# Packing the small experts of a mixture-of-experts layer, and one unsplit fp32 weight piece in six

## The reference

```
logits = h @ w_router + b_router                  # (256, 8)
top_logit, top_idx = top_k(logits, 2);  top_w = softmax(top_logit)
# for each expert e, over the rows xb of the tokens that chose it:
y_e = (silu(xb @ w1[e]) * (xb @ w3[e])) @ w2[e]   # w1, w3: 1024 x 3584, w2: 3584 x 1024
y[token] += top_w * y_e
```

## Time and profile before

| what | value |
|---|---|
| median of three runs | 1914.64 us |
| span of the profiled execution | 1919.3 us (no other time was recorded for it) |
| mean granted TensorE clock, share of full speed | 0.953 |
| TensorE matmuls busy | 1731.4 us, 90% |
| VectorE busy | 1421.4 us, 74% |
| ScalarE busy | 1042.3 us, 54% |
| read from HBM | 500.50 MB, 261 GB/s over the span |
| the experts' part | from 725.81 us to about 1900 us of the span |

### The profile page before, as it was taken

One profiled execution on the slowest core, in us unless ns is written; L12 is line 12 of the kernel. 1 busy time (PEld: TensorE's weight loads), 2 busy tenths in 40 slices (PEclk: granted clock), 3 DMA queues, 4 the chain that ended last, 5 costly groups with the idle time before them and its releaser, 6 DMA issues.

```text
span 1919.3 us, 22270 instructions
## 1 busy us (share of the span) xinstructions
PE 1731.4 (90%) x7882; PEld 1390.2 (72%) x7883; DVE 1421.4 (74%) x1201; ACT 1042.3 (54%) x817; POOL 25.5 (1%) x31
## 2 busy tenths in 40 slices
PE   1899979996999949989979989999899899999995
PEld 0787758885877727868868868887687687787784
DVE  7776877757676776877868866656588688787787
ACT  1465434433555326757747745554577576675773
POOL 0100000000000000000000000000000000000000
PEclk9998989998999969999999999999999999999998
DMA  9874458754665436987978965666599699799892
GB/s 367 309 271 144 154 186 315 275 182 171 249 214 179 145 115 240 357 327 274 362 288 306 363 253 197 219 219 219 180 354 380 236 362 363 278 359 344 300 362 83
DMA packets 210686, 503.98 MB, mean 263 GB/s; under 512 B 9137, under 2 KB 13409, under 8 KB 210481
## 3 DMA queue, kind: packets, MB, share of 16 engines
q1 hardware_dynamic: 208770, 496.15, 72.3%
q0 software_dynamic: 1712, 5.43, 0.9%
HBM read 500.50 MB, written 1.05 MB: 261 GB/s over the span
## 4 chain that ended last, share of the span: by engine, by line
PE 79%; DVE 10%; issue 8%; ACT 2%; DMA 1%; DVEq 0%; ACTq 0%; SPq 0%
PE ps L1241 22%; PE ps L1243 22%; PE ps L1242 22%; DVE w_lo L772 2%; PE ps L1247 2%; PE ps L1248 2%; PE ps L1644 2%; PE ps L1530 2%; PE ps L1686 1%; DVE mod_acc L797 1%; ACT w_hi L457 1%; DVE stats L817 1%; PE ps L1365 1%; DVE gates L966 1%; PE ps L1366 1%
## 5 line engine op out<-in xcount | busy, mean ns | idle before, releaser
L772 DVE TENSOR_TENSOR w_lo<-w_raw,w_hi 128x2048 fp32r<-128x2048 f32 x423 | 966.4, 2291 | 381.7 <-ACT w_hi L457 381.1
L457 ACT CAST w_hi<-w_raw 128x2048 fp32r<-128x2048 f32 x423 | 806.5, 1910 | 352.0 <-PE ps L1243 282.7
L1241 PE MATMUL ps<-w_hi,actT_hi 128*128 128x512 f32 (+1 forms) x1536 | 613.8, 400 | 60.0 <-issue 40.2
L1243 PE MATMUL ps<-w_hi,actT_lo 128*128 128x512 f32 (+1 forms) x1536 | 600.0, 391 | 0.0
L1242 PE MATMUL ps<-w_lo,actT_hi 128*128 128x512 f32 (+1 forms) x1536 | 599.4, 390 | 0.0
L1241 PEld LDWEIGHTS ps<-w_hi,actT_hi 128*128 128x128 f32 x1536 | 294.3, 192 | 132.3 <-issue 60.9
L1243 PEld LDWEIGHTS ps<-w_hi,actT_lo 128*128 128x128 f32 x1536 | 293.3, 191 | 61.6
L1242 PEld LDWEIGHTS ps<-w_lo,actT_hi 128*128 128x128 f32 x1536 | 294.8, 192 | 57.5 <-issue 1.0
L1241 PE MATMUL ps<-w_hi,gT_hi 128*128 128x512 f32 x536 | 213.1, 398 | 16.3 <-DVE gT_lo L1058 14.1
L1243 PE MATMUL ps<-w_hi,gT_lo 128*128 128x512 f32 x536 | 213.6, 398 | 0.0
L1242 PE MATMUL ps<-w_lo,gT_hi 128*128 128x512 f32 x536 | 213.2, 398 | 0.0
(11 more groups left out here) (225 smaller groups left out, 1070.3 us busy)
## 6 DMA issues: line engine op xcount, KB each, us to landing
w_raw<-in_exp_w_dram SPq DMA_DIRECT2D x336, 1024.0 KB, 7.0
w_raw<-in_ffn_w_dram SPq DMA_DIRECT2D x33, 1024.0 KB, 5.2
w_raw<-in_w_mod_mix_dram SPq DMA_DIRECT2D x24, 1024.0 KB, 8.1
w_raw<-in_w_mod_ffn_dram SPq DMA_DIRECT2D x24, 1024.0 KB, 5.3
w_raw<-in_w_gate_dram SPq DMA_DIRECT2D x24, 1024.0 KB, 5.7
w_raw<-in_w_in_dram SPq DMA_DIRECT2D x14, 1024.0 KB, 7.3
w_raw<-in_w_out_dram SPq DMA_DIRECT2D x8, 1024.0 KB, 5.1
w_raw<-in_w_branch_c_dram SPq DMA_DIRECT2D x4, 1024.0 KB, 5.0
```

What stands on the lines that cost most here:

```text
L457: nc.scalar.copy(w_hi[:, j % SPLIT, :], w_raw[:, i % RING, :]).then_inc(split_hi, 1)
L772: TTn(w_lo[:, j % SPLIT, :], w_raw[:, i % RING, :], w_hi[:, j % SPLIT, :].bitcast(F32), ALU.subtract).then_inc(piece_used, 1)
L1241: MM(to, hi, w_h, start=first, stop=False)
L1243: return MM(to, lo, w_h, start=False, stop=last)
```

## The change

- An expert of at most 64 rows gets one packed block (`fb=0`): the code for the folded block, before only for the second of two blocks, takes the block's number `fb`.
- In such an expert the second B piece of each panel (`WHOLE`, pieces 3, 7, 13, 19, 25, 31 and 37) is not split: TensorE multiplies w_raw itself, as fp32, by x_whole = x_hi + x_lo (64 columns and 64 zeros), four matmuls (`up_whole`). x_whole lies in mod_acc, is made by VectorE at the expert's start, and stands ahead of `packed_ready`, for which TensorE waits.
- SyncE waits for `split_used`, raised by TensorE, ahead of each load that goes into the slot of a `WHOLE` piece, in every expert.
- The gather of a second block moves from the end of the expert before into the expert's own start, and its branch on the next count is gone. A branch on a count of at most 64 is added.

```diff
+WHOLE = {i for i, piece in enumerate(EXPERT.pieces) if piece[0] == "B" and piece[2] == 1}
...
+        x_whole = mod_acc[:, 0:KD * P].rearrange("p (k q) -> p k q", k=KD)
...
             def stream(stretch, base, layer, expert=None, mod_layer=None, gap=0):
...
+                    if stretch is EXPERT and (i - RING) % EXPERT.n in WHOLE:
+                        sp.wait_ge(split_used, expert * EXPERT.n_split + (moe_splits + i - RING + 1 + SPLIT))
+                        load(i % RING, piece, layer, expert)
+                        continue
...
# ScalarE (VectorE alike)
-                    def round_expert_piece(i, e):
-
+                    def round_expert_piece(i, e, whole=()):
+                        if i in whole:
+                            return
+                        count = 2 if i - 1 in whole else 1
...
-                    def second_block(e, n):
-                        with act.If(act.value_load(counts_i[0:1, bass.ds(e, 1)], min_val=0, max_val=SEQ) > P):
-                            gathered_rows(1, n)
-                        with act.Else():
-                            act.sem_inc(xg_hi_ready[1], 1)
...
+                            if blocks == 2:
+                                gathered_rows(1, e + 1)
+                            else:
+                                act.sem_inc(xg_hi_ready[1], 1)
...
# VectorE
+                    dve.wait_ge(gate1_ready, 4)
+                    nc.vector.memset(x_whole[:, :, HALF_P:P], 0.0)
...
-                                dve.wait_ge(xg_hi_ready[1], e + 1)
-                                dve.wait_ge(xg_lo_ready[1], e + 1)
-                                nc.vector.tensor_copy(actT_hi[:, :, P + HALF_P:2 * P], actT_lo[:, :, P:P + HALF_P].bitcast(F32)).then_inc(packed_ready, 1)
+                                dve.wait_ge(xg_hi_ready[fb], e + 1)
+                                dve.wait_ge(xg_lo_ready[fb], e + 1)
+                                at = fb * P
+                                ins = nc.vector.tensor_copy(actT_hi[:, :, at + HALF_P:at + P], actT_lo[:, :, at:at + HALF_P].bitcast(F32))
+                                if fb == 0:
+                                    ins = TTn(x_whole[:, :, 0:HALF_P], actT_hi[:, :, 0:HALF_P].bitcast(F32), actT_lo[:, :, 0:HALF_P].bitcast(F32), ALU.add)
+                                ins.then_inc(packed_ready, 1)
...
# TensorE
+                    def up_whole(i, h):
+                        for k in range(4 * h, 4 * h + 4):
+                            ins = MM(bank(HW3), x_whole[:, k, :], w_raw[:, i % RING, (k % 4) * BANK:(k % 4 + 1) * BANK], start=k == 0, stop=k == KD - 1)
+                        return ins
...
-                        pe.wait_ge(piece_used, piece_base + i + 1 + RING)
+                        whole = fb == 0 and i in WHOLE
+                        if whole:
+                            pe.wait_ge(raw_loaded[i % RING], e * EXPERT.landed[i % RING] + (moe_loads[i % RING] + stretch.loads[i]))
+                        else:
+                            pe.wait_ge(piece_used, piece_base + i + 1 + RING)
...
-                        def expert(blocks, packed=False):
-                            if packed:
+                        def expert(blocks, fb=None):
+                            pe.wait_ge(xg_hi_ready[0], e + 1)
+                            pe.wait_ge(xg_lo_ready[0], e + 1)
+                            if blocks == 2:
+                                gather(1, e + 1)
+                                pe.wait_ge(xg_hi_ready[1], e + 1)
+                                pe.wait_ge(xg_lo_ready[1], e + 1)
+                            else:
+                                pe.sem_inc(gathered_hi[1], 1)
+                                pe.sem_inc(gathered_lo[1], 1)
+                            if fb is not None:
                                 pe.wait_ge(packed_ready, e + 1)
...
-                            expert(1)
+                            with pe.If(count > HALF_P):
+                                expert(1)
+                            with pe.Else():
+                                expert(1, fb=0)
```

More of the change, by code:

```diff
@@ L173 @@
 FOLDS = 2 * len(EXPERT_PANELS)
+WHOLE = {i for i, piece in enumerate(EXPERT.pieces) if piece[0] == "B" and piece[2] == 1}
+assert EXPERT.n - 1 not in WHOLE and not WHOLE & set(range(SPLIT))
 LOGITS = 64
@@ L631, in _, with panel_events @@
                                             sbase + MIX.n_split))
-                def panel_events(stretch, panels, split_base, panel0, blocks, folds=None):
+                def panel_events(stretch, panels, split_base, panel0, blocks, folds=None, fb=None):
+                    whole = [b for b in range(blocks) if b != fb]
                     first_b = {stretch.split_no[i]: p[1] for i, p in enumerate(stretch.pieces) if p[0] == "B" and p[2] == 0}
@@ L643, in gT_part @@
                         for b in range(blocks):
-                            n = HALF_P if b and folds is not None else P
+                            n = HALF_P if b == fb else P
                             ins = A(gT_hi[:, b, 0:w // P, 0:n], ps[:, HW1 + 2 * b, 0:w].rearrange("p (c q) -> p c q", q=P)[:, :, 0:n], ACT.Copy)
@@ L655, in after @@
                             if folds is not None:
-                                A(fold[:, 0, 0:w], ps[HALF_P:P, HW1 + 2, 0:w], ACT.Copy).then_inc(fold_copied, 1)
-                            for b in range(1 if folds is not None else blocks):
+                                A(fold[:, 0, 0:w], ps[HALF_P:P, HW1 + 2 * fb, 0:w], ACT.Copy).then_inc(fold_copied, 1)
+                            for b in whole:
                                 ins = A(silu[:, b, 0:w], ps[:, HW1 + 2 * b, 0:w], ACT.Silu)
@@ L1082, in after @@
                                 dve.wait_ge(fold_added, folds + 2 * p + 2)
-                                ins = TTn(gated[0:HALF_P, 1, 0:w], silu[0:HALF_P, 1, 0:w], fold[:, 1, 0:w], ALU.mult)
+                                ins = TTn(gated[0:HALF_P, fb, 0:w], silu[0:HALF_P, fb, 0:w], fold[:, 1, 0:w], ALU.mult)
                             ins.then_inc(gated_ready, 1)
@@ L1219, in _ @@
                             with dve.Else():
-                                expert(2, packed=True)
+                                expert(2, fb=1)
                         with dve.Else():
-                            expert(1)
+                            with dve.If(count > HALF_P):
+                                expert(1)
+                            with dve.Else():
+                                expert(1, fb=0)
                     dve.wait_ge(added, 4 * EXPERTS + 4)
@@ L1520, in _, with swiglu @@
                 open_sublayer(layer * 2 + 1, 0, 4)
-                def swiglu(stretch, panels, piece_base, panel0, blocks, e=None, turn_places=None, packed=False):
+                def swiglu(stretch, panels, piece_base, panel0, blocks, e=None, turn_places=None, fb=None):
                     def turn(p):
@@ L1527, in turn @@
                         for b in range(blocks):
-                            n = HALF_P if b and packed else P
+                            n = HALF_P if b and b == fb else P
                             for c in range(panels[p] // P):
@@ L1546, in down @@
                             for n in range(2):
-                                ins = (packed_product if b and packed else product)(
+                                ins = (packed_product if b == fb else product)(
                                     bank(2 * b + n), gT_hi[:, b, k, :], gT_lo[:, b, k, :], *split_piece(j, c, n * BANK, D),
```

90 lines of the change are left out of this document (39 added, 51 removed).

## The result

The changed kernel takes 1965.38 us (median of four, 1961.73 to 1967.34) where the kernel before takes 1914.67 (1905.44 to 1916.42) on the same chip: a ratio of 1.0275, 95% interval 1.0246 to 1.0304. That is slower, and past the range of the prediction. The profiled spans are 1965.7 and 1919.3 us: 46.3 us to explain.

The account below looks back on a forecast made before the run. It took TensorE to set the pace, with VectorE's ring next in small experts. Terms -21 + 12 + 4 + 1 = -4 us took the profile from 1919.3 to 1915, or 1911 us from the median; range 1888 to 1939.

Parts of the forecast that it names:

- Added at the loop's turn: Start of each small expert: TensorE waits for VectorE's turn, copy and x_whole, some 7.4 us idle; +12 us in all.
- rival 2: Start of each small expert: VectorE comes round late, in 10.79 us instead of 4.89; +27, 1938 us; chance 0.14.
- The removed branch: Loop's turn: dropping the second block's branch saves between nothing and 5.9 us of ScalarE's turn; taken as nothing.
- Expert 3: Start of the two-block expert: second gather now stands behind TensorE's turn; +4 us, bounds +1 and +6.
- SyncE's wait: Loads into a whole piece's slot, every expert: SyncE waits for that piece's product, later loads behind it; +1 us.
- The ring: Panel of a small expert: ScalarE's handshake, VectorE and one TensorE piece set a 16.43 us period, gaining 0.56 a panel.
- Rivals 3 and 4: Small experts' panels: transfers hold them at 16.99 us, 1928, chance 0.13; or more overlap shortens them to 15.7, 1890, chance 0.15.
- The small expert: Each of five experts of at most 64 rows: 4.2 us saved, -21 us together.
- The start: Small expert, restart until the end of panel 1's second A piece: 16.4 us after that loss-laden beginning; gain 1.8.
- The panels: Small expert, five periods to panel 6: gain 2.8 us, less 1.2 for the token picks.
- The end: Small expert's last panel from the second A on: 20.1 us before, 20.2 after; gain taken as 0.8.
- rival 1: Small experts' panels: TensorE's gaps lower the granted clock once a panel; +39, 1950 us; chance 0.08.

Follow-up runs that it names:

- Run 2: The changed kernel with its test count > HALF_P made count > 0, so the third body stays in the code but is never taken: 1963.59 us, ratio 1.0242.
- run 5: The changed kernel without its third body, all experts of up to 128 rows using the ordinary one-block body; later second gather and SyncE's wait stay: 1937.35 us.
- run 12: The changed kernel with packing in the previous expert's tail, the loop's closing branch announced and the small body tested for first: 1895.84 us, ratio 0.9895.
- run 14: The kernel of run 12 with VectorE's picks of the next expert's tokens moved from the middle panel to the tail: 1886.92 us, ratio 0.984.

## Why the prediction was wrong

**The failed step is "Added at the loop's turn".** It gave the small experts +12 us (its five costs add up to 12.6); their idle times, 25.4 us before (2.56, 8.20, 4.86, 7.02 and 2.73), are 68.6 now, +43, of which 40 are loss (expert 0 starts only 3.4 us later, though its idle time grew by 6.7). Two prices were wrong in it.
- *VectorE's turn.* "VectorE took 4.89 us to come round to the same copy before expert 3". That row was not near enough: expert 3's body comes early in the code, and that turn had two far jumps, 2.75 and 1.97 us. The way to a small expert has three, the first of them longer; the same copy follows the last addition after 12.49 us. This is the mechanism of rival 2, which had the right place and, at 1938, a price 27 us too low. It took ScalarE's turn of 10.79 us as the worst case, and that was a turn of a kernel with one body fewer.
- *TensorE's own turn.* It had no term at all. I took its idle times as a property of the loop that the change leaves alone. Run 2 shows 12.5 us with nothing of the change in use but the third body. With early packing TensorE's own way is 9.4 to 13.2 us, so even a VectorE that came round in 4.89 us would not have saved the forecast.

The two far jumps of VectorE on its way into expert 3, from the chain of waits of the kernel before:

```profile
1139.07 2.75 issue
...
1142.71 1.97 issue
```

Of the 50 us between the forecast's -4 and the 46.3 of the trace, 28 are this step at the small experts, 16 the small experts themselves, 4 expert 3 and 2 experts 1 and 6.

The rows to price it were in the trace: ScalarE's 10.79 us and TensorE's 8.20 us "waiting for nothing that the profile shows" each stood behind taken branches, and the queues of instructions were on the page.

**The removed branch** of the second block was priced at nothing, since it was ScalarE's. In run 5, which lacks it, the short gaps are gone; that the one is the cause of the other is not shown. Why the kernel before has gaps of 2.7 and 2.9 us at some turns and 7 to 8 at others, with the same path through the code, isn't settled; the former need one block of code for TensorE and the latter three.

**Expert 3**: +4 forecast, 5.5 measured in the gap (10.2 to 15.7, the gather cold at 7.08 us, as its upper bound had it) and 2.8 in the expert itself. **SyncE's wait**: +1 forecast, about nothing measured.

**The ring** held as a mechanism. With 0 at 1045.24, the forecast put the silu at 1.55, the first split at 2.08, VectorE's at 4.02, gT at 6.23 and TensorE's first C at 6.78; the trace has 1.54, 2.08, 4.06, 6.27 and 6.83. The whole piece takes 3.60 us, where 3.65 was forecast. The period is 16.75 instead of 16.43 us: VectorE's multiplication waits 0.2 us for its own fold, and the eight matmuls of a piece take 0.1 us more behind a gap. So the gain is 0.24 us a period, not 0.56. Rivals 3 and 4 are out: the transfers run at 388 GB/s in such a panel, no engine waits there for a landing, and no panel was shorter than 16.7.

**The small expert**: -4.2 us each forecast, -1.0 measured. I cut the five where the prediction cut them, at the end of the second A piece of panel 1 and of panel 6.
- The start holds: -8.6 us, where -9 was forecast. It takes 16.5 to 17.6 us, and 15.0 where the turn is clean (run 12, experts 2, 5 and 7), against the 16.4 forecast.
- The panels are 3.2 us longer instead of 8 shorter. The period gives 0.24 us and not 0.56; the first one takes 17.3 us, since VectorE adds the fold of panel 1 only after other work (the silu is 2.1 us behind the end of the A piece there, not 1.54); and the picks cost 1.2 us in two experts and 2.4 in three, where 1.2 was forecast, the rest by the clock. Before, they were not hidden either: that panel took 17.7 us instead of 17.0.
- The end is 0.3 us longer instead of 4 shorter.

With the turn and the picks out of the way (run 14) the sum comes near the forecast: 3.8 us each against the kernel before. That is luck in part: the start gives 3.4, the panels 1.2 and the end takes 0.8, where 1.8, 1.6 and 0.8 gained were forecast.

**The clock** (rival 1) did not fall once a panel: the period is 16.7 to 16.8 us in all five. Between them it fell only behind the picks, where TensorE is idle for 2.62 us, in three experts of five: 0.83 over 10 us in expert 4, 1.00 in expert 2 behind the same 2.62.

## What to carry to other kernels

In a loop whose bodies are chosen at run time, a body more is not free when it isn't taken: count the far jumps of every engine from the end of one body to the start of the next, and price each by the "issue" steps behind branches and by the packets of the instruction queues. Here the body that is taken most belonged first, the closing branch wanted its hint, and work that another engine had to finish before the next iteration belonged ahead of the turn. Before new work is put on an engine that has slack, ask whether the change makes that engine the ring, and move what else it does there.

## What was not expected of the hardware

- A far jump costs 2.0 to 7.3 us (VectorE 1.97 in the kernel before, 2.38, 3.56 and 5.99 in the kernel after; ScalarE up to 7.33 there), with 16 KB packets for what I take for TensorE and 8 KB for the others.
- With the closing branch announced, five of seven gaps of the kernel before became none (8.2 us before expert 2), though 13 of the 35 us came back inside the experts.
- Idle time of 2.62 us of TensorE lowered the granted clock in three experts of five and not in the others, with the same work before it.
